# Moving the memory-key products ahead of the memory queries, and one set of transposes ahead of the last diagonal product, in a two-layer block

## What is computed

```python
# layer 1: attention over the memory (4 heads of 128)
y_c = memory_attention(qm, rmsnorm(mem, g_mem[l]), w_mem_kv[l]) @ w_mem_out[l]
# layer 2: SSD branch, 4 groups (G), 4 chunks of 128 positions
y_diag = jnp.einsum('bclsgj,bcsgjp->bclgjp', cb[..., None] * decay, xdt)
y_off = jnp.einsum('bclgn,bcgjpn->bclgjp', cm, prev) * jnp.exp(a_cum)[..., None].astype(xs.dtype)
y = (y_diag + y_off + xs * d_skip.reshape(G, J)[:, :, None].astype(xs.dtype)).reshape(b, s, SSD_D_INNER)
yz = (y * jax.nn.silu(z)).reshape(b, s, G, SSD_D_INNER // G)
return rms_norm(yz, ssd_norm_g.reshape(G, -1))
```

## Time and profile before

| | |
|---|---|
| median of 3 runs | 2191.9 us |
| the profiled execution | 2191.61 us |
| its span in the trace | 2189.8 us |
| busy: TensorE, VectorE, ScalarE, GpSimd | 92%, 45%, 32%, 10% |
| mean granted clock of TensorE | 0.969 |

### The profile page before, as it was taken

One profiled execution on the slowest core, in us unless ns is written; L12 is line 12 of the kernel. 1 busy time (PEld: TensorE's weight loads), 2 busy tenths in 40 slices (PEclk: granted clock), 3 DMA queues, 4 the chain that ended last, 5 costly groups with the idle time before them and its releaser, 6 DMA issues.

```text
span 2189.8 us, 23017 instructions
## 1 busy us (share of the span) xinstructions
PE 2022.6 (92%) x9514; PEld 1408.9 (64%) x9514; DVE 994.8 (45%) x1558; ACT 701.7 (32%) x1122; POOL 218.7 (10%) x281
## 2 busy tenths in 40 slices
PE   7999999997999999899999999999995988888886
PEld 6777788896888788777777765666593332322332
DVE  4457434436666523677888436652245111111113
ACT  4343423324444312554555323552121100100100
POOL 2000000001000000001111012110023111111110
PEclk9999999998999999999999999999996999999999
DMA  7241222333222322332223221112229999999995
GB/s 261 87 135 58 77 79 95 113 138 106 96 97 96 135 96 96 106 123 89 73 97 120 86 78 58 58 58 77 77 107 399 413 423 424 422 423 420 419 413 219
DMA packets 56856, 380.43 MB, mean 174 GB/s; under 512 B 12936, under 2 KB 13192, under 8 KB 23856
## 3 DMA queue, kind: packets, MB, share of 16 engines
q1 hardware_dynamic: 38304, 339.23, 39.9%
q0 software_dynamic: 17872, 38.68, 5.1%
q10 hardware_dynamic: 576, 1.05, 0.2%
HBM read 378.82 MB, written 27.89 MB: 186 GB/s over the span
## 4 chain that ended last, share of the span: by engine, by line
PE 69%; DMA 18%; DVE 9%; ACT 2%; POOL 1%; issue 1%; SPq 0%; DVEq 0%; POOLq 0%; ACTq 0%
PE PS L490 17%; PE PS L491 17%; PE PS L492 17%; DMA AR<-in_wexp 16%; PE PS L1080 5%; PE PS L873 4%; PE PS L537 3%; DVE AR L1462 1%; PE PS L486 1%; PE PS L850 1%; POOL AR L2398 1%; PE PS L1103 1%; PE PS L906 1%; PE PS L938 1%; DVE AR L1455 0%
## 5 line engine op out<-in xcount | busy, mean ns | idle before, releaser
L490 PE MATMUL PS<-rf,rf 128*128 128x512 f32 (+1 forms) x1896 | 724.0, 382 | 11.1 <-DVE rf L1122 6.4
L492 PE MATMUL PS<-rf,rf 128*128 128x512 f32 (+1 forms) x1896 | 711.1, 375 | 0.0
L491 PE MATMUL PS<-rf,rf 128*128 128x512 f32 (+1 forms) x1896 | 711.1, 375 | 0.0
L1122 DVE TENSOR_TENSOR rf<-AR,rf 128x1024 fp32r<-128x1024 f32 (+1 forms) x210 | 268.6, 1285 | 385.6 <-ACT rf L1939 385.5
L490 PEld LDWEIGHTS PS<-rf,rf 128*128 128x128 f32 x1896 | 359.6, 190 | 84.7 <-issue 14.9
L492 PEld LDWEIGHTS PS<-rf,rf 128*128 128x128 f32 x1896 | 359.2, 189 | 64.8
L491 PEld LDWEIGHTS PS<-rf,rf 128*128 128x128 f32 x1896 | 359.4, 190 | 63.9 <-issue 3.1
L1939 ACT ACTIVATE rf<-AR 128x1024 fp32r<-128x1024 f32 (+1 forms) x210 | 229.5, 1102 | 292.7 <-PE PS L492 195.0
L1080 PE MATMUL PS<-AR 128*64 128x512 f32 x1024 | 272.2, 639 | 50.9 <-DMA AR<-in_wexp 49.2
L1080 PEld LDWEIGHTS PS<-AR 128*64 128x64 f32 x1024 | 85.7, 147 | 231.6 <-issue 156.6
L1884 DVE TENSOR_TENSOR AR<-AR,PS 128x256 f32<-128x256 f32 x32 | 13.5, 421 | 359.2 <-ACT AR L2384 359.2
(11 more groups left out here) (327 smaller groups left out, 1836.7 us busy)
## 6 DMA issues: line engine op xcount, KB each, us to landing
AR<-in_wexp SPq DMA_DIRECT2D x62, 2048.0 KB, 35.9
AR<-in_wpack SPq DMA_DIRECT2D x123, 1024.0 KB, 5.0
AR<-in_wexp SPq DMA_DIRECT2D x68, 1024.0 KB, 38.1
AR<-acud POOLq DMA_DIRECT2D x16, 512.0 KB, 4.1
AR<-ya SPq DMA_DIRECT2D x4, 1024.0 KB, 7.9
bvec<-bv POOLq DMA_DIRECT2D x1, 2560.0 KB, 16.2
AR<-in_x SPq DMA_DIRECT2D x4, 512.0 KB, 7.2
AR<-bvec POOLq DMA_DIRECT2D x8, 256.0 KB, 2.9
```

The costliest lines, as they stand in the source:

```text
L490: e.i.matmul(o, ws[0], xs[0], start=start, stop=False)
L491: e.i.matmul(o, ws[0], xs[1], start=False, stop=False)
L492: return e.i.matmul(o, ws[1], xs[0], start=False, stop=stop)
L1122: e.i.tensor_tensor(rounded(p.place + p.width, p.width), src, rounded(p.place, p.width).bitcast(F32), ALU.subtract).then_inc(*tick("w_lo", ...
```

## The change

There are two edits, with no new arithmetic.

In the first layer `mk` and `mv` come ahead of `qm`: in the order of the weights, and in the dense steps of TensorE, VectorE and ScalarE. `mv` also has a step of its own now, so that there is one dense step more.

In the SSD branch `turn(g, 2)` moves from behind the first convolution tile of the next group to a place ahead of `yd(g, 3)`. The other three of each group stay where they were.

The order of the weights:

```diff
-    first = names("t", "q", "k", "v", "qm", "mk", "mv", "cc", "cv", "cb")
+    first = names("t", "q", "k", "v", "mk", "mv", "qm", "cc", "cv", "cb")
```

TensorE's dense steps of the first layer (the old branch for `mk` inside the loop over names goes):

```diff
-                for name in ("qm", "mk", "cc", "cv", "cb"):
+                for j in range(4):
+                    tile("mk", j, NM, ("v_out" if j % 2 else "a_out", ("mk", j)), 256)
+                    if j % 2:
+                        yield
+                rows("mv", NM, 2, lambda i: ("a_out", ("mv", i)))
+                yield
+                for name in ("qm", "cc", "cv", "cb"):
                     for j in range(4):
```

TensorE's program in the SSD branch:

```diff
+            todo = None
             for g in range(4):
                 for j in range(4):
                     conv_tile(f"xs{g}", j, 4 * g + j)
                     if j:
                         xs_rows(g, j - 1)
-                    if j < 2 and g:
-                        turn(g - 1, 2 + j)
+                    if j == 1 and todo:
+                        turn(*todo)
+                        todo = None
...
-                    if c in (1, 2):
-                        turn(g, c - 1)
+                    if todo:
+                        turn(*todo)
                     b, was = banks.take(("yd", g, c), ("v_out", ("yd", g, c)))
...
                     m.then_inc(*tick("acc", ("yd", g, c)))
+                    todo = (g, c)
```

ScalarE's dense steps (VectorE's alike, without the copies; behind them both go on with `qm` and `cc`):

```diff
                 for j in range(4):
                     projected_one("mk", j, MK, 256)
-                    if j == 3:
-                        for u in range(4):
-                            ahead("mv", u)
-                        for i in range(2):
-                            e.wait_ge(*at("acc", ("mv", i)))
-                            e.i.activation(MV[:, i, :], ps(("mv", i)), ACT.Copy).then_inc(*tick("a_out", ("mv", i)))
                     if j % 2:
                         yield
+                for u in range(4):
+                    ahead("mv", u)
+                for i in range(2):
+                    e.wait_ge(*at("acc", ("mv", i)))
+                    e.i.activation(MV[:, i, :], ps(("mv", i)), ACT.Copy).then_inc(*tick("a_out", ("mv", i)))
+                yield
```

More of the change, by code:

```diff
@@ L684, in dense_1 @@
             def dense_1():
-                for name in ("qm", "mk", "cc", "cv", "cb"):
-                    for j in range(4):
-                        if name == "mk":
-                            tile("mk", j, NM, ("v_out" if j % 2 else "a_out", ("mk", j)), 256)
-                            if j == 3:
[L690 to L693, removed]
+                for j in range(4):
[5 more added lines that the diff above has]
+                for name in ("qm", "cc", "cv", "cb"):
+                    for j in range(4):
                         back = {"cv": ("v_out", ("cv", j)), "cb": ("v_out", ("ab", j))}
@@ L852, in tensor @@
                     m.then_inc(*tick("acc", ("yd", g, c)))
[L854 to L858, removed]
+                    todo = (g, c)
+            rows("q0", N3, 4, lambda i: ("a_out", ("q0", i)), lambda: turn(*todo))
             rows("q1", N3, 4, lambda i: ("a_out", ("q1", i)))
@@ L1275, in dense_1 @@
                 for j in range(4):
-                    projected_one("qm", j, QM)
-                    yield
-                for j in range(4):
                     projected_one("mk", j, MK, 256)
-                    if j == 3:
-                        for u in range(4):
-                            ahead("mv", u)
                     if j % 2:
                         yield
-                for j in range(4):
-                    projected_one("cc", j, CCB)
-                    yield
+                for u in range(4):
+                    ahead("mv", u)
+                yield
+                for name, dst in (("qm", QM), ("cc", CCB)):
+                    for j in range(4):
+                        projected_one(name, j, dst)
+                        yield
                 for j in range(4):
@@ L2243, in scalar @@
                 if u == 1:
-                    turn(3, 2)
-                    turn(3, 3)
+                    turn(*todo)
             e.wait_ge(*at("v_out", "ang"))
```

## The result

The changed kernel takes 2210.65 us (median of 4 runs, 2208.57 to 2211.89) against 2193.05 us for the kernel before (2191.61 to 2195.18): 1.0079 times as long, 95% interval 1.0061 to 1.0096, some 17 us. The forecast was slower by 13, so the direction and the places were right and the size was short by about 4 us. The time lies above the range around my sum (2198 to 2208), at the upper edge of the wide one (2210.5), and closest to the rival *dear clock* (2208.3 to 2210.3), to which I had given 8%. The profiled execution spans 2206.6 us, 16.8 more than that of before. The runs of the kernel before fall into two groups, near 2191 and near 2195 us, and its profiled one is of the first.

The account below looks back on a forecast made before the run. TensorE, busy 92% of the span, was taken as the bound. The profiled 2191.6 us + 4.0 (first layer) + 9.2 (SSD branch) = 2204.8, forecast 2205.0 us; range 2198 to 2208, widened to 2195.5 to 2210.5.

Parts of the forecast that it names:

- dear clock: Rival, both edits: every clock restart costs 3.0 us, the first-layer edit +6; 2208.3 us, or 2210.3 with split waits; 8%.
- the wide one: Range for the whole kernel's time, widened to take in the edges of rivals: 2195.5 to 2210.5 us.
- Forecast waits 1.7 + 4.9 + 1.8: First layer: TensorE waits at mv's start, at mv's last part and at the first qm tile, 8.4 us in all.
- 1.1 for the clock: First layer: low clock left over behind the 4.9 us wait, taken from between 0 and 3.0 us.
- edit 1 is free: Rival, first layer: mv's part 3 is split in time, old waits and low clock vanish, -5.5 us; 2195.6 us; 10%.
- 2.3 for each group with the transposes: SSD branch: yd and all behind it come 2.3 us later in each of four groups, +9.2 us.
- I took no change: SSD branch: clock restarts cost the same in all as before, 10.8 us; -4.4 and +1.2 kept for the range.
- The bound of 3.0: SSD branch: highest price of one clock restart, read from group 1; 1.6 was the lowest.
- its bound of 12.0 us for four restarts: SSD branch: upper end of the four clock restarts together, 6.4 to 12.0 us.
- stages behind the SSD branch keep their length: Behind the SSD branch: every stage is as long as before, so the experts start later by both edits' sum.
- ScalarE's splits move with TensorE: SSD branch: ScalarE's later weight splits shift along with TensorE, with one copy less in front; costed at nothing.

Follow-up runs that it names:

- e1: The kernel before with only mk and mv ahead of qm, the SSD branch left as it was: 2198.2 us, ratio 1.0019.
- e5: e1 with the split of the last part of mv put ahead of the exponentials and maxima of heads 2 and 3: 2190.2 us, ratio 0.9985.
- e3: The kernel before with turn(g,2) directly behind yd(g,3), ahead of the next group's first tile: 2194.8 us, ratio 1.0002.
- e12: e2 with four extra matmuls per group that compute nothing, between of and the moved transposes: 2193.5 us, ratio 0.9996.
- e4: The kernel before with the next group's first convolution tile between of and yd of chunk 3, groups 0 to 2: 2205.2 us, ratio 1.0053.
- e8: The changed kernel with the next group's first convolution tile ahead of the moved transposes, groups 0 to 2: 2210.4 us, ratio 1.0080.
- e11: e5 with the earlier splits of e6 but without its tile ahead of yd: 2190.3 us, ratio 0.9984.
- e6: e5 with the tile of e4 and the next group's gate and third-tile weight splits earlier on ScalarE and VectorE: 2187.9 us, ratio 0.9978.
- e2: The kernel before with only turn(g,2) moved ahead of yd(g,3), the first layer left as it was: 2205.8 us, ratio 1.0053.
- e9: e2 with GpSimd's d_skip product for the next chunk ahead of its reciprocal root: 2205.1 us, ratio 1.0055.

## Why the prediction was right, and where it was short

**Edit 1, by its steps.** Forecast waits 1.7 + 4.9 + 1.8, measured 1.46 + 4.72 and none: the third was hidden in the slow 12 matmuls, as the step said that slow work before 125.6 would be, and the first `qm` tile began at 126.24, which is 125.67 on the forecast's scale (the stretch begins 0.57 us later in this execution), against 125.6. The first column grew by 2.9 us where I had added 1.1 for the clock to the same 2.9; e1's +4.2 (2.2 to 6.1 by its interval) can't tell 2.9 from 4.0. The rival "edit 1 is free" is out. e5 shows that its mechanism exists, one split away.

**Edit 2, the wait.** Forecast: idle 4.5 us in place of 2.3, 2.3 for each group with the transposes, 9.2 in all. Measured: 4.55 for 2.31, +9.0 in the waits. e3 confirms that the transposes themselves cost nothing.

**Edit 2, the clock: the term that was mis-sized.** I took no change and gave -4.4 to +1.2 for the range, with a restart at 1.6 to 3.0 us. By the timelines (transposes, `yd` and tiles behind it against their usual spacing) the four restarts cost 3.3, 3.0, 2.9 and 1.5 us before, 10.7 together, and 3.3, 3.5, 3.6 and 3.7 after, 14.1 together: +3.4. In group 1: 0.89 for the transposes instead of 0.44, 3.27 instead of 1.71 for `yd`, 12.66 instead of 11.12 for two tiles. The bound of 3.0 came from one group, in which the transposes weren't part of the slow stretch and the idle time was half as long. The Trainium skill, "TensorE: Matmul & The Clock Gate", section "HAM oscillation — how this bites in real kernels", has such a loop pay in every pass; the trace agrees, with 3.3 to 3.7 us in all four groups. e12 shows the mechanism, since without the idle time the clock stayed full.

Of the rivals, *dear clock* was thus right about the SSD branch, and even its bound of 12.0 us for four restarts was too low. It was wrong about edit 1, which cost 2.9 us and not 6, and no tile of the next group waited for a split that hadn't been waited for before. That its sum comes closest to the measured time is in part luck.

**The sum.** 2.9 + 9.0 + 3.4 = 15.3 us; the two profiled spans differ by 16.8. The 1.8 of the feed-forward stage more than fill the rest; the same two values come in kernels that have none of the edits in that place, so I count it as the scatter of single executions, and of the 4 us by which the forecast was short about half is this and not a term of the sum. That stages behind the SSD branch keep their length was right: from the first product of `so` to the first product of the experts it is 386.0 us before and 385.9 after, so the experts start 17.2 us later.

**What the prediction didn't see** is the chain behind `yd`. That ScalarE's splits move with TensorE is true of the order as it was; but 5.6 us of useful work ahead of `yd` costs 11 us in e4, and in e8 it gains nothing, since as much waiting comes back behind `yd` as it takes away ahead of it.

**Open:** what decides how long the clock stays low behind one and the same wait. In the fourth group before it was low for half as long as in the others, and began only behind `yd`, which took 1.78 us up to the next product and not 3.40. Kernels with the same order there have group distances of 67.3 to 68.9 us, and the waits of 2.6 us in the feed-forward stage, 2.7 in the first layer and 2.1 ahead of `so` each brought the low clock in some kernels and none in others.

## What to carry to other kernels

Before a step with a wait is moved ahead of others on an in-order engine, follow its input's chain to the end: moving the consumer doesn't bring the producer forward, and all that stands behind it inherits the rest of the wait. On TensorE allow for the restart of the clock behind such a wait: here it cost 1.5 to 3.7 us beside 2.3 to 4.6 of waiting, though waits of 2.1 to 2.7 us in other stages brought none in some kernels. Filling a wait with work only pays if the chain that starts behind it isn't the next one to bind (e4), and which one binds is seen when both halves are tried apart (e4, e11) and together (e6). A gain or loss of 1 to 2 us in one stage of one trace can be the clock alone, so look at the granted clock there before giving it to an edit.

## What the runs showed of the hardware

Four products of 0.86 us that compute nothing made a kernel 12.3 us faster, though the wait that they fill ended no earlier: with them the granted clock was 1.00 in the stretch where it is 0.79 in the changed kernel. A wait of 1.0 us left behind them brought no low clock. Two orders of GpSimd's and VectorE's steps cost the same: a GpSimd product (1.04 us in e2, 1.55 in e9) lengthened whichever VectorE instruction lay beside it, `fn` from 0.75 to 1.52 us or the two `em` from 1.28 to 2.13.

The clock also gives a stage more than one length. Behind the same wait of 2.7 us the granted clock was 0.83 over 10 us in one kernel and 1.00 in another, and the same happened behind one of 2.6 and one of 2.1 us; each time it made 1.6 to 1.8 us.
